# Attention levels of a hybrid decoder step: products and masked copies for the odd blocks' queries only

## The reference

```
G = cumsum(log f)                      # per channel
decay[t, s] = exp(G[t] - G[s])         # for s <= t, per channel
att[t, s] = sum_k q[t, k] * decay[t, s, k] * k[s, k]
o = att @ v + (q * exp(G)) @ S
```

## Time and profile before

| what | value |
| --- | --- |
| median of three runs | 1838.98 us |
| lowest and highest run | 1836.88, 1843.45 us |
| the profiled execution | 1840.96 us |
| its span from first to last instruction | 1838.9 us |
| PE busy | 1486.7 us (81%), 7565 instructions |
| DVE busy | 566.0 us (31%), 1407 instructions |
| mean granted clock of TensorE | 0.912 |

### The profile page before, as it was taken

One profiled execution on the slowest core, in us unless ns is written; L12 is line 12 of the kernel. 1 busy time (PEld: TensorE's weight loads), 2 busy tenths in 40 slices (PEclk: granted clock), 3 DMA queues, 4 the chain that ended last, 5 costly groups with the idle time before them and its releaser, 6 DMA issues.

```text
span 1838.9 us, 19426 instructions
## 1 busy us (share of the span) xinstructions
PE 1486.7 (81%) x7565; PEld 839.3 (46%) x7565; DVE 566.0 (31%) x1407; ACT 285.2 (16%) x565; POOL 296.1 (16%) x402
## 2 busy tenths in 40 slices
PE   6899999798989996878787788788787787777870
PEld 5677776577758773433233233233233232233330
DVE  2779999666651223101010010010010010010015
ACT  2111111333320001111111011011011011011111
POOL 0066665333200000000000000000000000000006
PEclk9899999999979997988988998888999998899895
DMA  9324242335317625999999999999999999999964
GB/s 284 117 92 138 92 138 92 116 118 163 108 29 230 229 92 193 395 398 393 378 382 369 377 384 387 381 376 372 383 370 373 380 378 376 372 387 390 367 241 151
DMA packets 253055, 505.27 MB, mean 275 GB/s; under 512 B 23572, under 2 KB 99556, under 8 KB 233708
## 3 DMA queue, kind: packets, MB, share of 16 engines
q1 hardware_dynamic: 235788, 493.74, 74.5%
q0 software_dynamic: 5200, 9.19, 1.6%
q10 hardware_dynamic: 12016, 1.66, 0.6%
HBM read 503.18 MB, written 26.28 MB: 288 GB/s over the span
## 4 chain that ended last, share of the span: by engine, by line
DMA 35%; PE 26%; SPq 6%; DVE 1%; POOL 1%; issue 1%; ACT 0%; POOLq 0%; ACTq 0%; DVEq 0%
DMA ring<-in_w_up_dram 34%; PE bank L1261 16%; SPq L384 6%; PE bank L1191 6%; PE bank L1282 1%; PE bank L900 1%; DMA ring<-expert_rows 0%; PE bank L1158 0%; PE bank L1141 0%; POOL arena L862 0%; POOL arena L863 0%; PE bank L1169 0%; DVE arena L1798 0%; PE bank L1211 0%; PE bank L1228 0%
## 5 line engine op out<-in xcount | busy, mean ns | idle before, releaser
L1261 PE MATMUL bank<-ring,arena 128*64 128x512 f32 x2048 | 518.8, 664 | 156.8 <-DMA ring<-in_w_up_dram 156.8
L1261 PEld LDWEIGHTS bank<-ring,arena 128*64 128x64 f32 x2048 | 196.4, 152 | 452.6 <-issue 452.6
L1282 PE MATMUL bank<-ring,arena 128*64 128x512 f32 x1024 | 259.8, 666 | 19.0 <-DVE arena L1785 19.0
L1780 DVE SCALAR_TENSOR_TENSOR arena<-arena,gcol 64x512 f32<-64x512 f32 x32 | 23.8, 743 | 728.8 <-ACT arena L727 728.8
L930 PE MATMUL bank<-arena,ring 128*128 128x280 f32 x768 | 188.8, 405 | 3.0 <-ACT arena L579 1.9
L930 PEld LDWEIGHTS bank<-arena,ring 128*128 128x128 f32 x768 | 145.9, 192 | 44.1 <-issue 7.6
L1282 PEld LDWEIGHTS bank<-ring,arena 128*64 128x64 f32 x1024 | 80.5, 152 | 174.6 <-issue 174.6
L839 POOL DMA_INDIRECT expert_rows<-arena,idx_dst x32 | 29.5, 922 | 800.2 <-ACT arena L732 800.2
L732 ACT ACTIVATE arena<-bank 64x512 f32<-64x512 f32 x128 | 75.9, 593 | 330.0 <-PE bank L1282 328.8
L1191 PE MATMUL bank<-ring,arena 128*128 128x256 f32 x512 | 114.8, 386 | 0.0
L1228 PE MATMUL bank<-ident,arena 64*128 64x64 f32 x721 | 66.3, 239 | 56.7 <-DVE arena L1780 47.5
(11 more groups left out here) (333 smaller groups left out, 1403.9 us busy)
## 6 DMA issues: line engine op xcount, KB each, us to landing
ring<-in_w_down_dram SPq DMA_DIRECT2D x64, 2048.0 KB, 21.2
ring<-in_w_gate_dram SPq DMA_DIRECT2D x64, 2048.0 KB, 19.6
ring<-in_w_up_dram SPq DMA_DIRECT2D x64, 2048.0 KB, 22.6
ring<-in_w_in_dram SPq DMA_DIRECT2D x20, 2048.0 KB, 8.7
ring<-in_w_out_dram SPq DMA_DIRECT2D x8, 2048.0 KB, 9.7
ring<-in_s_w_glu_dram SPq DMA_DIRECT2D x2, 2048.0 KB, 8.4
arena<-v_samples SPq DMA_DIRECT2D x8, 512.0 KB, 4.4
ring<-expert_rows SPq DMA_DIRECT2D x4, 1024.0 KB, 9.3
```

The source lines that it names most:

```text
L1261: ins = pe.matmul(PB[b][at:at + CAP, :], xgT[b][:, kk, :], slot(s, KD // 2)[:, k, :], start=(kk == 0), stop=(kk == KD - 1))
L1282: ins = pe.matmul(PB[2 + cc // 2][at:at + CAP, :], hT[:, f, :], slot(4 + half, KF // 2)[:, k, cc * 512:(cc + 1) * 512], start=(f == 0), st ...
```

## The change

At levels 0 to 6 the streamed operand and the output of the product are no longer the whole chunk but its odd blocks: 64 of 128 columns, 8 of 16 (from level 3). In level l these are runs of B columns with gaps of B between them, from one run of 64 to 64 runs of one. The weights remain the whole chunk. The masked copies read mask and PSUM and write `att[b]` in the same columns. Level 7 is as before, as are the number and order of instructions and all waits. The columns of even blocks in the bank are not written any more, and not read.

```diff
+        def odd_blocks(v, l):
+            return v.rearrange("p (n two b) -> p n two b", two=2, b=LV[l])[:, :, 1, :]
...
                     for c0, n_ in (CHUNKS if l >= 3 else CHUNKS[:2]):
+                        out = bank[0:n_, c0:c0 + n_]
                         if l < 7:
-                            k_ = q_ = QK[b][:, LO[l] + c0:LO[l] + c0 + n_]
+                            k_ = QK[b][:, LO[l] + c0:LO[l] + c0 + n_]
+                            out, q_ = odd_blocks(out, l), odd_blocks(k_, l)
                         else:
                             k_, q_ = kT[:, h, c0:c0 + n_], qT[:, h, c0:c0 + n_]
-                        ins = pe.matmul(bank[0:n_, c0:c0 + n_], k_, q_, start=True, stop=True)
+                        ins = pe.matmul(out, k_, q_, start=True, stop=True)
...
-                    ins = nc.vector.copy_predicated(att[b][:, 0:2 * P].rearrange("p (a n) -> p a n", a=2),
-                                                    masks[:, l, :].unsqueeze(1).broadcast_to([P, 2, P]),
-                                                    bank[:, 0:2 * P].rearrange("p (a n) -> p a n", a=2))
-                    if l >= 3:
-                        ins = nc.vector.copy_predicated(att[b][0:LAST, 2 * P:TP], masks[0:LAST, l, 0:LAST],
-                                                        bank[0:LAST, 2 * P:TP])
+                    if l < 7:
+                        pair = [v.rearrange("p (a n two b) -> p a n two b", a=2, two=2, b=LV[l])[:, :, :, 1, :]
+                                for v in (att[b][:, 0:2 * P], bank[:, 0:2 * P])]
+                        mask = odd_blocks(masks[:, l, :], l)
+                        ins = nc.vector.copy_predicated(pair[0], mask.unsqueeze(1).broadcast_to([P, 2] + list(mask.shape[1:])), pair[1])
+                        last = [odd_blocks(v, l) for v in (att[b][0:LAST, 2 * P:TP], masks[0:LAST, l, 0:LAST],
+                                                           bank[0:LAST, 2 * P:TP])] if l >= 3 else None
+                    else:
...
+                    if last is not None:
+                        ins = nc.vector.copy_predicated(last[0], last[1], last[2])
```

More of the change, by code:

```diff
@@ L1558, in _ @@
                     bank = PB[4 + l % 2]
-                    ins = nc.vector.copy_predicated(att[b][:, 0:2 * P].rearrange("p (a n) -> p a n", a=2),
-                                                    masks[:, l, :].unsqueeze(1).broadcast_to([P, 2, P]),
-                                                    bank[:, 0:2 * P].rearrange("p (a n) -> p a n", a=2))
-                    if l >= 3:
-                        ins = nc.vector.copy_predicated(att[b][0:LAST, 2 * P:TP], masks[0:LAST, l, 0:LAST],
-                                                        bank[0:LAST, 2 * P:TP])
+                    if l < 7:
[6 more added lines that the diff above has]
+                    else:
+                        ins = nc.vector.copy_predicated(att[b][:, 0:2 * P].rearrange("p (a n) -> p a n", a=2),
+                                                        masks[:, l, :].unsqueeze(1).broadcast_to([P, 2, P]),
+                                                        bank[:, 0:2 * P].rearrange("p (a n) -> p a n", a=2))
+                        last = [att[b][0:LAST, 2 * P:TP], masks[0:LAST, l, 0:LAST], bank[0:LAST, 2 * P:TP]]
+                    if last is not None:
+                        ins = nc.vector.copy_predicated(last[0], last[1], last[2])
                     ins.then_inc(att_read, 1)
```

## The result

The change made the kernel slower: 1846.62 us against 1839.33 us, medians of eleven runs each, ratio 1.0036 with a 95% interval of 1.0025 to 1.0047. The forecast was 1837.1 us, and the time lies above its range of 1831 to 1845 us. One execution of a later run, e1, was disturbed (2182.91 us, mean granted clock 0.637) and is left out of its figures. The profiled execution took 1849.12 us (span 1847.1), 8.16 more than that of before.

The account below looks back on a forecast made before the run. TensorE's half of each head's loop was taken to set the pace. Saving 0.060 us in each of four levels of eight heads, 1.9 us, from the median 1838.98 gave 1837.1 us, range 1831 to 1845.

Parts of the forecast that it names:

- What bounds the heads: Head loop: TensorE's half of 14.26 us in a 22.04 us period sets the pace; VectorE waits within it.
- the pass: Product at levels 0 to 6: a 64-column pass costs its weight load, 0.11 us, so nothing is saved between passes.
- the size change: Levels 3 to 6, where weights change between 128 and 16 columns: 0.060 us saved in each level.
- the strided columns: Product on TensorE: columns with gaps cost 0.84 ns each, as now.
- The first rival: Product passes: the stream, not the load, sets the pass, 0.111 to 0.072 us; 10.7 us saved, 1828.3; chance 0.08.
- The second: Strided columns slow TensorE's product: levels 1 to 6, 1860 us, chance 0.08; or level 6 alone, 1841.1, chance 0.07.
- The copies at nothing: Masked copies: 9 us less of VectorE's time, nothing on the path, since idle ahead of them grows.
- the bound of a doubled price: Masked copies: if strided PSUM reads doubled an element's price, a copy takes as long as now, behind the same idle.
- The sum over eight heads: Levels 3 to 6 of all heads: 8 x 4 x 0.060 = 1.9 us saved, 0.24 us in the last head too.
- The rival on the clock: Levels of the heads: TensorE streams less and its clock falls, five dips of 1.7 us loss each, 1845.6; chance 0.05.

Follow-up runs that it names:

- e1: Kernel before with only the products put on odd blocks, masked copies over all 128 columns: 1843.48 us, 1.0014 of before.
- e5: Changed kernel, but products stream and write the first 64 (8) neighbouring columns of each chunk instead of odd blocks: 1843.3 us, 1.0017 of before.
- e2: Kernel before with only the masked copies put on odd blocks, products over all 128 columns: 1840.17 us, 0.9997 of before.
- e3: Changed kernel, but products over all 128 columns in the last head: 1837.29 us, 0.9985 of before.
- e6: Changed kernel, but each odd block streamed twice, so 128 columns with gaps in the operand and the whole bank written: 1840.92 us, 1.0003 of before.
- e8: Kernel before plus five unused 280-column products in the last head's TensorE wait for ScalarE: 1837.85 us, 0.9990 of before.
- e7: Changed kernel plus five unused 280-column products in the last head's TensorE wait for ScalarE: 1835.92 us, 0.9978 of before.
- e10: The changed kernel measured again, unaltered: 1843.70 us, 1.0020 of the kernel before.
- e4: Changed kernel, but products over all 128 columns in heads 0 to 6, odd blocks in the last head alone: 1845.43 us, 1.0030 of before.

## Why the prediction was wrong, point by point

**What bounds the heads, the pass, the size change, the strided columns: right.** TensorE's half sets the pace; a 64-column pass costs its weight load, since the loads follow each other at 0.11 us as before and levels 0 to 2 kept 1.39 us; levels 3 to 6 fell to 1.67; the period fell by 0.23 us against 0.24. The first rival is out, as levels 0 to 2 show. The second is out in both forms: levels 5 and 6 take 1.67 us like level 3, and e5, without gaps, has the period of the changed kernel (21.81 and 21.82 us). The Trainium skill, "Advanced Engine Details and Errata", section PSUM Cachelines, says that patterns with gaps slow matmuls; for these fp32 products the runs do not bear it out, by the levels and the periods just named.

**The copies at nothing: right.** e2 is the kernel before to within 0.15%. At two of the seven levels the copies did reach the bound of a doubled price (below), behind the idle that was named.

**The sum over eight heads: wrong in the eighth.** The step that failed is the sentence that in the last head "0.24 us is saved there as well". It took the 2.01 us of the earlier trace rows, a level at the full clock, for the level after the change too. It was 3.44, at half the clock. In the profiled execution the head lost 8.8 us where 0.24 were to be gained, more than the 1.3 that the other seven gave.

**The rival on the clock: the right resource, dismissed by the wrong reason.** It priced dips of 3.4 us in the middle heads, took the fall of the earlier trace rows as a sample of what a dip costs, and argued that idle stretches don't grow and TensorE remains occupied. Both hold in the two profiles: the wait is 2.35 us before and 2.41 after, and the middle heads kept 1.00. Dips of 3.4 us outside the last head do occur (e1, e3, and with 128 columns e2, e6, e8), but one to a profile and not five. The fall that mattered stood in the last head already, on the path, and the question was how long it would last once TensorE streams half as many columns in each product. Nor was 3.4 us the only sample: the trace of before has the fall of 20.4 us from 532.1 on, which the prediction doesn't name. Occupied was not enough: TensorE was busy for 24.82 of the 26.70 us from 513.3 to 540, at 0.50. The forecast had 0.05 for the clock, and that its price, 1845.6, lies near the result is luck; the range stopped short of it, at 1845.

**The size.** With the clock kept, e7 lies 1.9 us below e8 in medians, the whole forecast gain; the spread of their runs (up to 7.4 us) makes that agreement and no proof. The changed kernel lost 7.3 us in the first measurement and 3.7 in e10; in the one profiled execution of each its fall lasted 47.8 and 20.5 us. The Trainium skill, "TensorE: Matmul & The Clock Gate", section on HAM oscillation, describes a kernel whose clock falls again and again because TensorE waits between its bursts of matmuls. The traces agree in that the fall in the levels comes with the wait, in eight profiles of nine, and show besides that the return differs with the work behind the wait: 3.4 us in before, e2 and e6, 20.5 to 47.8 us in the changed kernel, e1, e5 and e10. e4, with 64 columns and 3.4 us, is the exception.

**What stays open:** why the clock came back early in the profiled execution of e4. Where the fall begins may bear on it, beside the columns: with 64 columns it began 0.1 to 1.4 us before the wait's end where it was long, and 0.8 us after it in e4; with 128 it began 0.04 us (e2, e6) and 0.6 us (before) after it. No run varied this by itself. Open are also what brings the falls in heads 4 and 6, and how much of the difference between e1's ratio and the changed kernel's is more than chance.

## What to carry to other kernels

Read every stretch in which the granted clock is below 1.00 as a piece of the path with a beginning and an end, and ask of a change what it does to both ends; making matmuls narrower can cost time where a fall already stands, though no wait grows and no matmul is slower by itself. Where TensorE must wait at such a place, matmuls that nobody reads can be the cheaper wait: five here turned a kernel 0.36% slower than before (0.20% in its second measurement) into one 0.22% faster, and eleven gave 0.30%. In the kernel before, the same five gave 0.10%, which is not clear of noise. And judge a small change in each stage separately, since the stage that repeats seven times and the one that comes once answered with opposite signs.

## What was not expected of the hardware

**A clock at half through nearly unbroken work.** TensorE left the wait at 514.14 and was busy for 24.81 of the 25.86 us to 540, yet the granted clock stayed at 0.50 throughout, and to 561. With 128 columns for 64 in otherwise the same instructions (e2, e6) it returned after 3.4 us. The kernel before has such a stretch too, on other work: busy for all of the 5.00 us from 532.1 on, with products of 8 and 16 columns among them, its TensorE stayed at 0.50.

**The masked copy's price goes by the length of the runs.** 128 elements take 0.29 to 0.30 us at levels 0 to 4 (runs of 64 to 4 elements), and 0.44 us at levels 5 and 6 (runs of 2 and 1), as long as 256 neighbouring ones took the earlier trace rows; the 16-token copy takes 0.15 and 0.20. It is so in every head, and in e2 as well, where the products have no gaps (levels 4 and 5):

```profile
411.76 0.29 DVE L1569 COPY_PREDICATED arena<-masks,bank 128x128 f32<-128x128 uint8 x1 [1.38 <-PE bank L1077]
...
413.49 0.44 DVE L1569 COPY_PREDICATED arena<-masks,bank 128x128 f32<-128x128 uint8 x1 [1.38 <-PE bank L1077]
413.73 0.20 DVE L1578 COPY_PREDICATED arena<-masks,bank 16x8 f32<-16x8 uint8 x1
```

Which of the three operands causes it, the PSUM read, the byte mask or the write, was not tried. VectorE's fp32 products on single elements did not show it.
